# Expert down weights loaded as 16 KB runs, with up and gate products that read every fourth weight column

## The chip, the cores and the metric

One core of a Trainium2 chip runs the whole program; the other cores are idle. The metric is the device time of one execution in microseconds (us), from the first to the last instruction. The core has a matrix engine (TensorE, PE in the profile, with its weight loads as PEld), a vector engine (DVE), a scalar engine (ACT), GpSimd (POOL) and SyncE (SP), which in this kernel issues nearly all transfers from the chip's memory into on-chip memory. A matmul here is called with a stationary operand (loaded into the array first) and a moving operand (streamed past it column by column).

## The reference

Two transformer layers on 256 tokens of width 1024, all in float32. The second one ends in a mixture of 32 experts with two experts for each token. Cut to what matters here:

```python
def expert_block(args):
    xb, e = args                       # tokens of expert e, 1024 wide
    hid = jax.nn.silu(xb @ w1[e]) * (xb @ w3[e])
    return hid @ w2[e]
...
"w1": (32, 1024, 512)   "w3": (32, 1024, 512)   "w2": (32, 512, 1024)     # float32
```

Each matrix of an expert is 2 MB, so the 96 matrices are 192 MB, and every one is read once. The hidden width is 512: hidden unit f is column f of w1 and w3 and row f of w2. The order in which the 512 hidden units are worked through is free as long as the columns of w1 and w3 and the rows of w2 agree on it.

## The kernel before, in words

The dense part of the two layers comes first (to about 690 us). After it the kernel routes the tokens and goes through the 32 experts in 8 quads of 4. For each quad it builds `xg`, the tokens of the four experts (up to 32 slots for each), by products of one-hot matrices with the normed tokens `n3` (line 977). There the stationary operand is `n3[:, tb, c:D:KC]`, which reads every eighth element of a row, 128 of them 32 bytes apart. Then, for each expert, with `places` the three on-chip places of its matrices:

- Lines 997 to 1002: for n = 0 (w1) and n = 1 (w3), 8 blocks c of the input width and 4 groups g of hidden units, a matmul whose stationary operand is 32 columns of `xg` and whose moving operand is a 128x128 piece of the weights. Group g uses its own 32 columns of the array (`tile_position`), and its result goes to its own 32 partitions of `ps`; the four groups run side by side. Each float32 matmul is recorded as two, so a matrix is 64 records of L999.
- ACT takes the silu (L1285), DVE multiplies (L1782), PE turns the result over (L1004), DVE copies it to `hid_T` (L1784).
- Lines 1007 to 1011: the down product with w2, in which block b of four takes the hidden units that group b of the step before has made: 32 records of L1009. ACT and DVE bring the result out (L1288, L1787).

At the end of a quad L1019 weights the results by the gates and puts them back to their tokens, and DVE adds them to `h` (L1793).

The weights come through `expert_load` on SP's queue (line 559), in the order w1, w3, w2 for expert 0, 1, 2 and so on. Expert 2 has places of its own (`third_w`); the others alternate between `even_w` and `odd_w`. SP issues w1 of expert e+2 when the w1 products of expert e are done (`e_w1`), w3 after its w3 products (`e_up`), and w2 after its down products (`e_y`); for expert 3 it waits for expert 0, and for expert 4 for expert 2. From expert 4 on this is the loop `stream`. w1 and w3 put rows 8p to 8p+7 on partition p, 16 KB that lie together in memory. w2 puts rows p, 128+p, 256+p and 384+p on partition p, four runs of 4 KB. An instruction whose weights have not landed waits in order on PE, and all that follows it on PE waits too.

Of the kernel before, what the change touches and what calls it, by code (L numbers as in the profile page):

```python
# [31 lines left out]
P = 128  # L32
# [16 lines left out]
EFF = 512  # L49
SLOTS = 32  # L50
# [206 lines left out]
def layers_kernel(nc, a, table, windows, out):  # L257
# [135 lines left out]
    xg = moe("xg", [P, KC, P])  # L393
# [123 lines left out]
    @block.sync  # L517
    def _(sp):
        def load(u):
            if u >= 3:  # L520
                sp.wait_ge(lo_ready, u - 2)
            kc, cols = units[u]["kc"], units[u]["cols"]
            dst = ring[:, u % 3, 0:kc * cols].rearrange("p (c n) -> p c n", c=kc)
            for c0, c1, src in units[u]["src"]:
                sp.dma_start(dst[:, :, c0:c1], src).then_inc(landed[u % 3], 16)

        for tb in range(TB):
            sp.dma_start(h[:, tb, :], a["x"][0, P * tb:P * tb + P, :]).then_inc(in_x[tb], 16)
        load(0)
        sp.wait_ge(in_rows, 80)  # L530
        load(1)
        sp.dma_start(mem_tok[:, :, :], a["mem"][0].rearrange("(b p) n -> p b n", p=P)).then_inc(in_mem, 16)
        for u in range(2, S2 + 3):
            load(u)

        up_v = a["w_ffn_in"][0].rearrange("(c p) n -> p c n", p=P)
        down_v = a["w_ffn_out"][0].rearrange("(c p) n -> p c n", p=P)
        with sp.Fori(2, NF - 1) as i:
            addresses = [sp.snap(i * UC), sp.snap(i * UC + FF), sp.snap(i * 2 - 2)]
            freed = [sp.snap(i * 3 + (S2 - 3 + j - 2)) for j in range(3)]  # L540
            for j in range(3):
                s = (S2 + j) % 3
                sp.wait_ge(lo_ready, freed[j])
                if j < 2:
                    dst = ring[:, s, :].rearrange("p (c n) -> p c n", c=KC)
                    src = up_v[:, :, bass.ds(addresses[j], UC)]
                else:
                    dst = ring[:, s, :].rearrange("p (c n) -> p c n", c=2)
                    src = down_v[:, bass.ds(addresses[j], 2), :]
                sp.dma_start(dst, src).then_inc(landed[s], 16)  # L550


        w1, w3, w2 = a["w1_2"][0], a["w3_2"][0], a["w2_2"][0]
        sources = (w1.rearrange("e (p c) f -> p e c f", c=KC), w3.rearrange("e (p c) f -> p e c f", c=KC),
                   w2.rearrange("e (c p) n -> p e c n", p=P))

        def expert_load(e, places, which, landing):
            src = sources[which][:, bass.ds(e, 1), :, :].rearrange("p e c n -> p (e c) n")
            sp.dma_start(places[which], src).then_inc(landing, 16)

        for u in range(S2 + 3 * (NF - 2), U):
            if u == second_merge + 2:
                sp.wait_ge(o_done, 20)
                expert_load(0, odd_w, 0, landed_w[1][0])
            elif u in (second_merge + 5, second_merge + 7):
                if u == second_merge + 5:
                    sp.wait_ge(o_done, 28)
                which = (u - second_merge - 3) // 2
                expert_load(0, odd_w, which, landed_w[1][which])
            load(u)  # L570
        sp.wait_ge(merged_ready, 8)
        expert_load(1, even_w, 0, landed_w[0][0])
        sp.wait_ge(lo_ready, U)
        expert_load(1, even_w, 1, landed_w[0][1])
        expert_load(1, even_w, 2, landed_w[0][2])
        sp.wait_ge(unit_done, U)
        for which in range(3):
            expert_load(2, third_w, which, in_third3[which])
        for which in range(3):
            sp.wait_ge((e_w1, e_up, e_y)[which], 1)  # L580
            expert_load(3, odd_w, which, landed_w[1][which])

        def stream(pass_, lo_pair):

            with sp.Fori(lo_pair, EXPERTS // 2) as i:
                for odd in range(2):
                    e = sp.snap(i * 2 + odd)
                    used = sp.snap(i * 2 + (pass_ * EXPERTS + odd - 1))
                    for which in range(3):
                        sp.wait_ge((e_w1, e_up, e_y)[which], used)  # L590
                        expert_load(e, (even_w, odd_w)[odd], which, landed_w[odd][which])

        stream(0, 2)
        sp.wait_ge(passes_ready, 1)
        n_pass = sp.value_load(passes_i[0:1, 0:1], min_val=1, max_val=T // SLOTS)
        with sp.If(n_pass > 1):
            with sp.Fori(1, n_pass) as again:
                stream(again, 0)
            sp.nop()
        for tb in range(TB):  # L600
            sp.wait_ge(fin_ready, tb + 1)
            sp.dma_start(out[0, P * tb:P * tb + P, :], n3[:, tb, :]).then_inc(fin_out, 16)
        sp.wait_ge(fin_out, 32)
# [62 lines left out]
    def _(pe):  # L666
# [190 lines left out]
        for step, *arg in plan:  # L857
# [63 lines left out]
            elif step == "rope":  # L921
# [4 lines left out]
                n = T if r == 0 else 2 * T  # L926
# [40 lines left out]
        def quad_body(q):  # L967

            looped = not isinstance(q, int)
            e0 = pe.snap(q * QUAD) if looped else 0  # L970

            if not looped:
                pe.wait_ge(n3_ready, 2)
            pe.wait_ge(hot_part, q * 2 + 2)
            for c in range(KC):
                for tb in range(TB):
                    last = mm(ps[:, 2 + c // 4, P * (c % 4):P * (c % 4) + P], n3[:, tb, c:D:KC],  # L977
                              one_hot[:, tb, :], start=tb == 0, stop=tb == 1)
            last.then_inc(xg_done, 1)
            pe.wait_ge(hot_ready, q + 1)  # L980
            for tb in range(TB):
                last = nc.tensor.transpose(ps[:, 0, P * tb:P * tb + P], gated_hot[:, tb, :], ident)
            last.then_inc(gt_done, 1)
            pe.wait_ge(xg_part, q + 1)
            pe.wait_ge(xg_ready, q + 1)
            for e in range(QUAD):
                if looped:
                    places, landing = (even_w, odd_w)[e % 2], landed_w[e % 2]
                    arrived = pe.snap(q * 32 + 8 * (e + e % 2))
                else:  # L990
                    places = (odd_w, even_w, third_w, odd_w)[e]
                    landing = (landed_w[1], landed_w[0], in_third3, landed_w[1])[e]
                    arrived = (16, 16, 16, 32)[e]
                done = pe.snap(e0 + e) if looped else e
                for n in range(2):
                    pe.wait_ge(landing[n], arrived)
                    for c in range(KC):
                        for g in range(4):
                            last = mm(ps[SLOTS * g:SLOTS * g + SLOTS, 4 + e % 2, P * n:P * n + P],  # L999
                                      xg[:, c, SLOTS * e:SLOTS * e + SLOTS], places[n][:, c, P * g:P * g + P],  # L1000
                                      start=c == 0, stop=c == KC - 1, tile_position=(0, SLOTS * g))
                    last.then_inc((e_w1, e_up)[n], 1)
                pe.wait_ge(e_hid, done + 1)
                nc.tensor.transpose(ps[:, 6, 0:P], hid[:, :], ident).then_inc(e_T, 1)  # L1004
                pe.wait_ge(landing[2], arrived)
                pe.wait_ge(e_hidT, done + 1)
                for b in range(4):
                    for g in range(4):
                        last = mm(ps[SLOTS * g:SLOTS * g + SLOTS, 7, 0:UC],  # L1009
                                  hid_T[:, SLOTS * b:SLOTS * b + SLOTS], places[2][:, b, UC * g:UC * g + UC],  # L1010
                                  start=b == 0, stop=b == 3, tile_position=(0, SLOTS * g))
                last.then_inc(e_y, 1)

            pe.wait_ge(gt_ready, q + 1)
            pe.wait_ge(e_yA, e0 * 2 + 2 * QUAD)
            pe.wait_ge(e_yD, e0 * 2 + 2 * QUAD)
            for tb in range(TB):
                for half in range(2):
                    last = mm(ps[:, 2 * tb + half, :], gate_T[:, P * tb:P * tb + P],  # L1019
                              y_quad[:, 512 * half:512 * half + 512], start=True, stop=True)  # L1020
                last.then_inc(comb_done, 1)

        quad_body(0)
        pe.wait_ge(passes_ready, 1)
        n_pass = pe.value_load(passes_i[0:1, 0:1], min_val=1, max_val=T // SLOTS)
# [818 lines left out]
```

## Time and profile before

| | |
|---|---|
| median of 3 runs | 1168.72 us (1168.04 to 1173.64) |
| span of the profiled execution | 1168.5 us |
| PE busy | 968.1 us, 83% |
| DVE busy, ACT busy | 525.2 us, 359.5 us |
| moved by DMA | 310.02 MB, 265 GB/s over the span |
| mean granted TensorE clock | 0.933 |

The profiled execution took 1168.5 us from its first to its last instruction, and no other time of it is recorded; that is 0.2 us under the median of the three runs. The busy times are shares of the whole span and say little of one stage: the dense part and the experts have different limits, so the views below are read by stretch. In the rows, "idle before <-" names what ended an engine's idle time before a group of instructions, and the clock is a share of 2.4 GHz.

### The profile page before, as it was taken

Reading aid. Unit: us, or ns where it says so; the run is one execution under the profiler, and the core shown is the slowest. Engines: PE = TensorE matmul, PEld = TensorE weight load, DVE = VectorE, ACT = ScalarE, POOL = GpSimd, SP = SyncE. Lnnn points to the kernel's source line nnn. Section 1 sums busy time; section 2 is a strip of 40 time slices with the busy share of each in tenths; the row PEclk is TensorE's granted clock in tenths of the full one; section 3 lists DMA queues with packets and bytes.
Section 4 is the critical chain, followed back from the end, with each engine's and each line's share of the span. In section 5 each row is a group of like instructions: output and inputs, shape, how many; then the busy total and the mean of one; then the engine's idle time right before and its main releaser. Section 6 shows DMA issues by size and latency. Waiting matters only on the chain.

```text
span 1168.5 us, 23578 instructions
## 1 busy us (share of the span) xinstructions
PE 968.1 (83%) x10387; PEld 854.4 (73%) x10387; DVE 525.2 (45%) x859; ACT 359.5 (31%) x541; POOL 46.3 (4%) x43
## 2 busy tenths in 40 slices
PE   5999999889999997999998877767676767676763
PEld 5999999889999996899987866645454545454542
DVE  4546666756555656778875641212121211111113
ACT  4445546453433335343665421010000000101001
POOL 0100000400000000000210200000000000000000
PEclk8999999989999999999999879999888888988897
DMA  9754423735555553544445886999999999999994
GB/s 331 223 179 145 132 70 97 241 129 190 192 177 196 179 179 118 164 144 155 145 145 185 268 340 260 391 404 421 422 422 424 422 423 422 422 422 422 422 422 167
DMA packets 121376, 310.02 MB, mean 265 GB/s; under 512 B 5636, under 2 KB 92360, under 8 KB 113000
## 3 DMA queue, kind: packets, MB, share of 16 engines
q1 hardware_dynamic: 119568, 304.66, 69.5%
q0 software_dynamic: 1008, 4.20, 1.0%
q8 instruction: 43, 0.70, 0.2%
q10 hardware_dynamic: 744, 0.35, 0.1%
q14 instruction: 13, 0.11, 0.0%
HBM read 308.14 MB, written 1.05 MB: 265 GB/s over the span
## 4 chain that ended last, share of the span: by engine, by line
PE 52%; issue 41%; DVE 3%; ACT 1%; DMA 1%; POOL 1%; ACTq 0%; POOLq 0%; DVEq 0%; SPq 0%
PE ps L671 16%; PE ps L672 15%; PE ps L673 15%; DMA arena<-in_w_proj_b 1%; PE ps L927 1%; DVE w_lo L1322 1%; PE ps L837 1%; PE ps L769 0%; PE ps L825 0%; PE ps L796 0%; DMA rows<-in_g_mix 0%; PE ps L800 0%; PE ps L815 0%; PE ps L804 0%; PE ps L803 0%
## 5 line engine op out<-in xcount | busy, mean ns | idle before, releaser
L671 PE MATMUL ps<-x_hi,w_hi 128*128 128x256 f32 x928 | 268.4, 289 | 0.0
L672 PE MATMUL ps<-x_lo,w_hi 128*128 128x256 f32 x928 | 263.7, 284 | 0.0
L673 PE MATMUL ps<-x_hi,w_lo 128*128 128x256 f32 x928 | 263.6, 284 | 0.0
L1322 DVE TENSOR_TENSOR w_lo<-arena,w_hi 128x2048 fp32r<-128x2048 f32 (+3 forms) x83 | 165.5, 1996 | 60.5 <-ACT w_hi L1064 60.0
L999 PE MATMUL ps<-arena,xg 128*32 128x128 f32 x3968 | 136.1, 298 | 64.3 <-DMA arena<-in_w 56.4
L671 PEld LDWEIGHTS ps<-x_hi,w_hi 128*128 128x128 f32 x928 | 178.1, 192 | 6.5 <-issue 4.9
L999 PEld LDWEIGHTS ps<-arena,xg 128*32 128x32 f32 x3968 | 121.7, 121 | 81.1 <-DMA arena<-in_w 67.9
L672 PEld LDWEIGHTS ps<-x_lo,w_hi 128*128 128x128 f32 x928 | 178.2, 192 | 1.6 <-issue 1.0
L673 PEld LDWEIGHTS ps<-x_hi,w_lo 128*128 128x128 f32 x928 | 178.1, 192 | 0.2
L1064 ACT ACTIVATE w_hi<-arena 128x2048 fp32r<-128x2048 f32 (+3 forms) x83 | 138.4, 1670 | 48.3 <-PE ps L673 26.2
L1782 DVE TENSOR_TENSOR hid<-silu_e,ps 128x128 f32<-128x128 f32 x32 | 9.2, 288 | 189.3 <-ACT silu_e L1285 189.3
L1009 PE MATMUL ps<-arena,hid_T 128*32 128x256 f32 x992 | 70.6, 433 | 26.5 <-DMA arena<-in_w 18.4
L671 PE MATMUL ps<-w_hi,x_hi 128*128 128x256 f32 x256 | 77.1, 301 | 12.2 <-DVE w_lo L1322 11.5
L977 PEld LDWEIGHTS ps<-one_hot,n 128*128 128x128 f32 x256 | 61.8, 337 | 25.1 <-DVE one_hot L1768 23.8
L977 PE MATMUL ps<-one_hot,n 128*128 128x128 f32 x256 | 63.3, 423 | 19.2 <-DVE one_hot L1768 19.2
L672 PE MATMUL ps<-w_lo,x_hi 128*128 128x256 f32 x256 | 75.1, 293 | 0.0
L673 PE MATMUL ps<-w_hi,x_lo 128*128 128x256 f32 x256 | 75.0, 293 | 0.0
L1009 PEld LDWEIGHTS ps<-arena,hid_T 128*32 128x32 f32 x992 | 35.6, 122 | 50.8 <-DMA arena<-in_w 23.1
L1332 DVE TENSOR_TENSOR w_lo<-arena,w_hi 128x2048 fp32r<-128x2048 f32 x24 | 55.0, 2293 | 31.2 <-ACT w_hi L1074 31.2
L1787 DVE COPY y_quad<-ps 32x256 f32<-32x256 f32 x64 | 27.2, 425 | 92.0 <-PE ps L1009 91.0
L1285 ACT ACTIVATE silu_e<-ps 128x128 f32<-128x128 f32 x32 | 8.9, 277 | 179.4 <-PE ps L999 179.4
L1288 ACT ACTIVATE y_quad<-ps 32x256 f32<-32x256 f32 x64 | 23.9, 373 | 124.9 <-PE ps L1009 124.2
(274 smaller groups left out, 1346.7 us busy)
## 6 DMA issues: line engine op xcount, KB each, us to landing
arena<-in_w SPq DMA_DIRECT2D x93, 2048.0 KB, 23.9
arena<-in_w_in SPq DMA_DIRECT2D x43, 1024.0 KB, 5.4
arena<-in_w_ffn_in SPq DMA_DIRECT2D x22, 1024.0 KB, 5.1
arena<-in_w_ffn_out SPq DMA_DIRECT2D x11, 1024.0 KB, 4.9
arena<-in_w_out SPq DMA_DIRECT2D x8, 1024.0 KB, 6.1
third_w<-in_w SPq DMA_DIRECT2D x3, 2048.0 KB, 12.8
arena<-in_w_mem_kv SPq DMA_DIRECT2D x2, 1024.0 KB, 5.8
arena<-in_w_pool_o SPq DMA_DIRECT2D x4, 512.0 KB, 3.3
```

The lines of the kernel that those rows point to most:

```text
L671: mm(dst, l_hi, r_hi, start=start, stop=False)
L672: mm(dst, l_hi, r_lo, start=False, stop=False)
L673: return mm(dst, l_lo, r_hi, start=False, stop=stop)
L837: mm(o[:, 0:T], v[:, 0, :], r[:, 0:T], start=True, stop=False)
L977: last = mm(ps[:, 2 + c // 4, P * (c % 4):P * (c % 4) + P], n3[:, tb, c:D:KC], one_hot[:, tb, :], start=tb == 0, stop=tb == 1)
L999: last = mm(ps[SLOTS * g:SLOTS * g + SLOTS, 4 + e % 2, P * n:P * n + P], xg[:, c, SLOTS * e:SLOTS * e + SLOTS], places[n][:, c, P * g:P * ...
L1009: last = mm(ps[SLOTS * g:SLOTS * g + SLOTS, 7, 0:UC], hid_T[:, SLOTS * b:SLOTS * b + SLOTS], places[2][:, b, UC * g:UC * g + UC], start=b ...
L1064: fn(w_hi[:, u % 3, 0:n], ring[:, u % 3, 0:n], ACT.Copy).then_inc(hi_ready, 1)
L1288: fn(y_quad[SLOTS * e:SLOTS * e + SLOTS, UC * g:UC * g + UC], ps[SLOTS * g:SLOTS * g + SLOTS, 7, 0:UC], ACT.Copy).then_inc(e_yA, 1)
L1322: v.tensor_tensor(w_lo[:, u % 3, 0:n], ring[:, u % 3, 0:n], w_hi[:, u % 3, 0:n].bitcast(F32), ALU.subtract).then_inc(lo_ready, 1)
L1332: v.tensor_tensor(w_lo[:, s, :], ring[:, s, :], w_hi[:, s, :].bitcast(F32), ALU.subtract)\
L1787: v.tensor_copy(y_quad[SLOTS * e:SLOTS * e + SLOTS, UC * g:UC * g + UC], ps[SLOTS * g:SLOTS * g + SLOTS, 7, 0:UC]).then_inc(e_yD, 1)
```

## The change

Two lines. `w2` is loaded with rows 4p to 4p+3 on partition p. Block b of partition p is then row 4p+b, so the hidden units of group g have to be g, g+4, g+8 and so on, and the moving operand of the up and gate products becomes `places[n][:, c, g:EFF:4]`: 128 float32 elements that lie 16 bytes apart.

```diff
         w1, w3, w2 = a["w1_2"][0], a["w3_2"][0], a["w2_2"][0]
         sources = (w1.rearrange("e (p c) f -> p e c f", c=KC), w3.rearrange("e (p c) f -> p e c f", c=KC),
-                   w2.rearrange("e (c p) n -> p e c n", p=P))
+                   w2.rearrange("e (p c) n -> p e c n", c=4))
...
                             last = mm(ps[SLOTS * g:SLOTS * g + SLOTS, 4 + e % 2, P * n:P * n + P],
-                                      xg[:, c, SLOTS * e:SLOTS * e + SLOTS], places[n][:, c, P * g:P * g + P],
+                                      xg[:, c, SLOTS * e:SLOTS * e + SLOTS], places[n][:, c, g:EFF:4],
                                       start=c == 0, stop=c == KC - 1, tile_position=(0, SLOTS * g))
```

No instruction is added, removed or moved on any engine. What changes on SP's queue is the shape of the w2 transfers. This is the piece with expert 1's last two matrices, expert 2's (`third_w_109` to `third_w_111`) and expert 3's; "-" is before, "+" is the change:

```order
-L559 DMA arena<-in_w_2 128x4096 x2
-L559 DMA arena<-in_w_2 128x4x1024
+L559 DMA arena<-in_w_2 128x4096 x3
 L559 DMA third_w_109<-in_w_2 128x4096
 L559 DMA third_w_110<-in_w_2 128x4096
-L559 DMA third_w_111<-in_w_2 128x4x1024
-L559 DMA arena<-in_w_2 128x4096 x2
-L559 DMA arena<-in_w_2 128x4x1024
+L559 DMA third_w_111<-in_w_2 128x4096
+L559 DMA arena<-in_w_2 128x4096 x3
```

Each w2 transfer was 128 partitions of 4 runs of 1024 elements, and becomes 128 runs of 4096 elements, the shape that w1 and w3 have. Its place in the queue is the same.

## Rows read from the trace of the kernel before

**Rows 1.** Busy time by stretch: engines, granted clock, DMA share, GB/s.

```profile
400.00:500.00 100.00, 92.58 (x655) 83.85 (x654) 64.31 (x79) 40.31 (x48) 1.92 (x3) 0.98 0.50 158
900.00:1000.00 100.00, 68.63 (x1114) 52.73 (x1110) 18.11 (x44) 8.62 (x24) 0.00 (x0) 0.88 1.01 422
```

**Rows 2.** DMA packets and SP's queue (q1) from 757 to 1150 us.

```profile
DMA packets 21323, 164.02 MB, mean 417 GB/s; under 512 B 1263, under 2 KB 1263, under 8 KB 14662
q1 hardware_dynamic: 21318, 163.94, 100.4%
```

**Rows 3.** Timeline of PE, 961 to 999 us: start, duration, instructions, idle before.

```profile
961.66 3.53 PE L999 MATMUL ps<-arena,xg 128*32 128x128 f32 x64 [2.97 <-DMA arena<-in_w]
966.57 1.95 PE L999 MATMUL ps<-arena,xg 128*32 128x128 f32 x64 [1.37 <-DMA arena<-in_w]
971.68 3.61 PE L1009 MATMUL ps<-arena,hid_T 128*32 128x256 f32 x32 [2.12 <-DMA arena<-in_w]
...
982.65 7.92 PE L977 MATMUL ps<-one_hot,n 128*128 128x128 f32 x32 [2.60 <-DVE one_hot L1768]
```

**Rows 4.** Timeline of PE, 912 to 940 us.

```profile
912.05 1.93 PE L1009 MATMUL ps<-arena,hid_T 128*32 128x256 f32 x32 [0.47 <-DMA arena<-in_w]
915.07 3.67 PE L1019 MATMUL ps<-y_quad,gate_T 128*128 128x512 f32 x8 [1.09 <-DVE y_quad L1787]
921.34 7.92 PE L977 MATMUL ps<-one_hot,n 128*128 128x128 f32 x32 [2.59 <-DVE one_hot L1768]
930.23 3.70 PE L999 MATMUL ps<-arena,xg 128*32 128x128 f32 x128 [0.76 <-DVE xg L1778]
935.45 1.93 PE L1009 MATMUL ps<-arena,hid_T 128*32 128x256 f32 x32 [0.47 <-DVE hid_T L1784]
937.17 3.71 PE L999 MATMUL ps<-arena,xg 128*32 128x128 f32 x128
```

**Rows 5.** Timeline of PE in the first two quads, 707 to 759 us.

```profile
707.58 3.70 PE L999 MATMUL ps<-arena,xg 128*32 128x128 f32 x128 [0.68 <-ACT xg L1280]
719.40 0.49 PE L999 MATMUL ps<-arena,xg 128*32 128x128 f32 x9 [1.40 <-issue]
727.79 1.50 PE L999 MATMUL ps<-third_w,xg 128*32 128x128 f32 x42 [2.08 <-issue]
734.67 2.38 PE L999 MATMUL ps<-arena,xg 128*32 128x128 f32 x76 [0.44 <-issue]
756.55 3.70 PE L999 MATMUL ps<-arena,xg 128*32 128x128 f32 x128 [0.76 <-DVE xg L1778]
```

**Rows 6.** Busy time by stretch, where SP's queue runs short.

```profile
756.00:758.00 2.00, 1.45 (x53) 1.45 (x57) 0.31 (x1) 0.48 (x2) 0.00 (x0) 1.00 0.80 324
758.00:760.00 2.00, 2.00 (x84) 1.98 (x75) 0.00 (x0) 0.00 (x0) 0.00 (x0) 1.00 0.74 158
760.00:762.00 2.00, 0.81 (x18) 0.34 (x10) 0.58 (x2) 0.28 (x1) 0.00 (x0) 1.00 0.61 221
```

**Rows 7.** The end, 1145 us to the last instruction.

```profile
1145.50 3.35 PE L999 MATMUL ps<-arena,xg 128*32 128x128 f32 x64 [2.96 <-DMA arena<-in_w]
1150.49 1.93 PE L1009 MATMUL ps<-arena,hid_T 128*32 128x256 f32 x32 [0.61 <-DMA arena<-in_w]
```

**Rows 8.** A strided stationary operand (L977), a packed one (L852): ns min/median/max; pace by stretch.

```profile
L977 PEld LDWEIGHTS ps<-one_hot,n x256: 312/337/342, 698.8 to 1109.1; 128*128 128x128 f32 x128
L977 PE MATMUL ps<-one_hot,n x256: 343/404/606, 698.8 to 1109.2; 128*128 128x128 f32 x128
L852 PEld LDWEIGHTS ps<-w_route,n3T x32: 186/193/334, 676.2 to 689.0; 128*128 128x128 f32 x32
L999 PE MATMUL ps<-arena,xg x3968: 270/273/422, 707.6 to 1148.4; 128*32 128x128 f32 x199
698.80:702.00 3.20, 3.20 (x13) 3.20 (x14) 1.03 (x6) 0.00 (x0) 0.00 (x0) 0.50 0.49 198
702.00:706.50 4.50, 4.50 (x20) 4.50 (x20) 0.00 (x0) 0.00 (x0) 0.00 (x0) 0.99 0.00 0
```

## The prediction

> **What bounds the kernel now.** I read the busy times by stretch first. In the dense part, 400 to 500 us, TensorE is busy 92.58 of 100 us and the DMA engines are half idle. In the experts, 900 to 1000 us, it is the reverse: TensorE is busy 68.63 us, and the DMA share is 1.01 at 422 GB/s [rows 1]. The change touches only the experts, so I read on there.
>
> The view of the DMA queues says what the stream is made of. From 757 to 1150 us SP's queue keeps the 16 engines 100.4% busy. 21323 - 14662 = 6661 packets have 8 KB or more: w1 and w3 of 26 experts, 52 transfers of 128 runs of 16 KB, are 6656. 14662 - 1263 = 13399 have 4 KB: w2 of 26 experts in 512 runs is 13312 [rows 2]. So a w2 transfer goes as 512 packets where w1 and w3 go as 128.
>
> The timeline of PE gives the time of each landing, because there PE sits idle until it. w1 lands at 961.66, w3 at 966.57 (4.91 us later), w2 at 971.68 (5.11 us later) [rows 3]. A w2 transfer of the same 2 MB takes 0.20 us more. Four experts take 971.68 - 912.05 = 59.63 us, or 14.91 each, from one fourth w2 to the next [rows 3, 4].
>
> How much room does TensorE have? Where it waits for no landing, a quad costs: 3.02 us from the last down product to L1019, 6.27 to L977, 8.89 to L999, then 6.94 for each of three experts, and 5.22 from the start of the fourth to its down product [rows 4]. The sum is 44.2 us against 59.6 of DMA. The 15.4 us of room is what any extra cost on L999 has to fit into, and a quad has 8 matrices in L999.
>
> Before the stream settles TensorE is the one that others wait for. From 707.58 to 756.55 us none of its idle times in L999 ends with a landing; three end with nothing that the profile shows (1.40 + 2.08 + 0.44 = 3.92 us) [rows 5]. SP may fetch w1 of expert 6 only when L999 has used up w1 of expert 4, about 1.85 us after 756.55. The DMA rate falls to 158 GB/s just then [rows 6]: a deficit against 422 of (98 + 264 + 201)/422 x 2 us = 2.7 us. So the stream's last 26 experts hang on nine matrices of L999: eight of quad 0 and one of quad 1.
>
> **The change, part by part.**
>
> w2 in 16 KB runs. It gets the shape of w1 and w3, so I price it at their interval: -0.20 us each. Of 32 transfers only those behind the restart count, 26: -5.2 us. The bounds are 0 (if the 0.20 comes from something other than the packets) and -6.4 (all 32). The stream has no other gap to close.
>
> The Trainium skill ("DMA: Bandwidth & Descriptors", "Why small descriptors are slow (HBM only)") charges some 3 cycles for each packet beside one for each 32 bytes. As an estimate from that page, four packets of 128 + 3 cycles against one of 512 + 3 is 1.7%, or 0.09 us, where the rows show 0.20; by the page the gain would be 2.3 us. The rows decide.
>
> The strided moving operand. Each of the 64 matrices of L999 is 16 rounds of four concurrent matmul records. Packed, 128 records take 3.70 us, the last about 0.27 of it, so a round takes (3.70 - 0.27)/31 = 0.11 us [rows 4, 8], 0.86 ns a column. No row has a strided moving operand. The nearest is L977, a strided stationary one of the same 128 float32 columns, 32 bytes apart instead of 16. Its weight load lasts 337 ns where the packed one of L852 lasts 193. Its pace, with 0.40 us for the last of 32, is (7.92 - 0.40)/31 = 243 ns [rows 3, 8], more than twice the 110 ns of a packed round. And that pace does not follow the clock: 13 in 3.20 us at 0.50, 20 in 4.50 us at 0.99 [rows 8]. So what limits it is the reading of the operand, not the array. That is why I expect the moving operand to pay too.
>
> Bounds for one round: 110 ns (free), 243 ns (the pace of the row), and 4 x 110 = 440 ns if the four streams compete and a fetch that now serves four neighbouring columns serves one. The nearest row is L977. Its step is twice as wide as ours, so I take from exactly twice the packed round (220 ns) to its own pace (243 ns), and the middle, 231 ns. For a matrix that is 16 x (231 - 110) = +1.94 us; for the ends +1.76 and +2.13.
>
> Does that fit? TensorE's quad becomes 44.2 + 8 x 1.94 = 59.7 us, DMA's 59.63 - 4 x 0.20 = 58.8. It no longer fits: the limit is (58.8 - 44.2)/8 = 1.82 us for a matrix. TensorE becomes the bound, barely, and the DMA saving is lost. Summed along TensorE alone, with d the extra for a matrix:
>
> - start of quad 1: 756.55 + 8d
> - six quads to the start of quad 7: 6 x (44.2 + 8d)
> - to the last down product: 3 x 6.94 + 5.22 + 8d = 26.0 + 8d
> - the end behind it, unchanged: 1168.5 - 1150.49 = 18.0 [rows 7]
>
> The sum is 1065.8 + 64d. With d = 1.94 that is 1190.0; the ends give 1178.4 and 1202.1. Part of the 3.92 us of unexplained gaps in quad 0 may vanish under longer matmuls. I take off half: 1188. The two buffers for each matrix do not run dry before that: at a quad's first w1 TensorE is 3.02 + 6.27 + 8.89 + 3.7 = 21.9 us behind the last w2, while two experts, 29.4 us of transfers, are still queued.
>
> The low end of the cost is set by DMA: 1168.5 + 9 x 1.76 - 5.2 = 1179.1, or 1175 without the gaps. What follows an L999 group (L1285, L1782, L1004) moves with it. At the very end, w3's last products have to be through before w2 lands. Now PE waits 0.61 us for that landing [rows 7]; the sums hold this. No addition, copy or semaphore changes.
>
> **Rivals.**
>
> *The stride is free (0.30).* For it: 0.86 ns a column is two cycles at 2.4 GHz, which may leave room to fetch, and 16 bytes is half of L977's step. Against it: L977 has the same room and still pays. Then only the packets count: 1168.5 - 5.2 = 1163.3. This is the case on the other side, and it decides where the nine early matrices cost less than the packets give: 9d < 5.2, d < 0.58 us, a round under 146 ns. The Trainium skill ("SBUF — State Buffer", "Door 1: The DMA port swizzle") speaks of 16-byte lines and says "how far you can stride for free depends on dtype: 4 fp32". Read literally a step of four is still free and this rival holds. The same note wants two hits on each line, which a step of four does not give; no row here has this step, and L977's agrees only that a wider one costs.
>
> *The streams compete (0.12).* For it: four groups read at once, and L977 reads alone. Against it: nothing in the trace shows such a limit on packed reads. A round of 440 ns gives d = 5.28 and 1065.8 + 64 x 5.28 = 1404 us.
>
> *A mild cost (0.08).* d between 0.2 and 1.4: TensorE's quad stays under DMA's and only quad 0 and the restart pay, 1168.5 + 9d - 5.2, so 1165 to 1176.
>
> *Neither edit shows (0.04).* The packets don't set the 0.20 and the stride is free: 1168.5.
>
> **How the numbers follow.** My forecast, a doubled or slightly more than doubled round, has 0.46, and 1175 to 1212 for its own range (1212 is a round of 254 ns, from adding L977's extra 144 ns). With the free case and the mild one that is 0.84; the range is 1161 to 1212 and leaves out the competing streams. The measurement tells about 0.5%, 5.8 us, from no change. The free case, at -5.4 against the median, lies at that bound: I split it 0.13 faster, 0.17 same. The mild case is 0.06 same, 0.02 slower; the one without effect 0.04 same. The forecast gives 0.45 slower and 0.01 same, the competing streams 0.12 slower. That is 0.13, 0.28 and 0.59. The sums are made against the span of 1168.5 us, 0.2 under the median.
>
> **What the profile of the changed kernel would show.** Packets under 8 KB between 757 and 1150 us gone but for about 1300, and w2 landing 4.9 us after w3 wherever PE waits for both. If the forecast holds, 64 records of L999 take about 3.8 us at the full clock and nearly the same at the lower one; L1004's wait for `hid` is unchanged; quad 1's first L999 starts near 770 us instead of 756.55; waits of L999 for landings nearly vanish after quad 2; the DMA share in the experts falls a little under 1. If 64 records still take 1.95 us, the free case is right. If they take 7 us, the streams compete. The forecast is wrong if a moving operand is fetched further ahead than a stationary one, or if a step of 16 bytes is not yet the step that costs.

## The result and the profile after

The changed kernel is slower: 1187.43 us median (1185.33 to 1190.03) against 1171.18, ratio 1.0146, 95% interval 1.0125 to 1.0167. (1171.18 is the median of four runs of the kernel before: the three of its table and a fourth at 1173.95.) Its profiled execution took 1187.64 us with a span of 1185.8, 17.3 over the span of before. A time of a run lies about 1.8 us above its span here and in every other run that has both on record. So the span of 1168.5 of before belongs to a time near 1170.3, by that difference, and isn't a time to set beside 1168.72.

The timeline of PE over one settled quad, the answer to [rows 3, 4], shows where that comes from:

```profile
827.10 7.56 PE L999 MATMUL ps<-arena,xg 128*32 128x128 f32 x128 [0.76 <-DVE xg L1778]
...
868.73 1.93 PE L1009 MATMUL ps<-arena,hid_T 128*32 128x256 f32 x32 [0.47 <-DVE hid_T L1784]
871.75 3.67 PE L1019 MATMUL ps<-y_quad,gate_T 128*128 128x512 f32 x8 [1.09 <-DVE y_quad L1787]
878.03 7.92 PE L977 MATMUL ps<-one_hot,n 128*128 128x128 f32 x32 [2.60 <-DVE one_hot L1768]
886.91 7.55 PE L999 MATMUL ps<-arena,xg 128*32 128x128 f32 x128 [0.75 <-DVE xg L1778]
895.96 1.93 PE L1009 MATMUL ps<-arena,hid_T 128*32 128x256 f32 x32 [0.47 <-DVE hid_T L1784]
```

The two matrices of an expert take 7.55 us in L999 where they took 3.70. L1019, L977 and L1009 take what they took. And no row names a landing any more: L1009 waits for `hid_T`, L977 for `one_hot`. The view of PE's waits from 757 to 1168 us says the same for all quads:

```profile
PE ps L1004 <- DVE hid L1782: 19.9, 28, 0.7
PE ps L977 <- DVE one_hot L1768: 18.0, 7, 2.6
PE ps L1009 <- DVE hid_T L1784: 13.3, 28, 0.5
PE ps L1019 <- DVE y_quad L1787: 6.5, 6, 1.1
PE ps L999 <- DVE xg L1778: 5.3, 7, 0.8
```

Before, the longest waits of L999 and L1009 were for landings [rows 3]; the same view of the kernel before, from 757 to 1150 us, has 74.2 us of them in all:

```profile
PE ps L999 <- DMA arena<-in_w: 56.4, 27, 3.0
PE ps L1009 <- DMA arena<-in_w: 17.8, 13, 2.2
```

Here there is none. TensorE sets the pace. From 900 to 1000 us it is busy 83.47 us instead of 68.63 [rows 1]; the DMA rate did not fall there, because the two now need nearly the same time for a quad:

```profile
900.00:1000.00 100.00, 83.47 (x1150) 59.11 (x1143) 18.00 (x45) 8.05 (x23) 0.00 (x0) 0.98 1.00 425
```

The DMA view from 757 to 1150 us, the answer to [rows 2], shows the 4 KB packets gone and the queue no longer full (97.9% for 100.4%):

```profile
DMA packets 11103, 161.73 MB, mean 412 GB/s; under 512 B 1232, under 2 KB 1232, under 8 KB 1232
q1 hardware_dynamic: 11097, 161.63, 97.9%
```

The first two quads and the last down product, the answer to [rows 5 to 7]: timeline of PE, and then busy time by stretch.

```profile
707.76 7.52 PE L999 MATMUL ps<-arena,xg 128*32 128x128 f32 x128 [0.68 <-ACT xg L1280]
718.52 7.57 PE L999 MATMUL ps<-arena,xg 128*32 128x128 f32 x128
767.32 7.56 PE L999 MATMUL ps<-arena,xg 128*32 128x128 f32 x128 [0.76 <-DVE xg L1778]
...
1167.80 1.93 PE L1009 MATMUL ps<-arena,hid_T 128*32 128x256 f32 x32 [0.47 <-DVE hid_T L1784]
```

```profile
764.00:766.00 2.00, 2.00 (x10) 2.00 (x10) 0.00 (x0) 0.00 (x0) 0.00 (x0) 1.00 0.33 139
766.00:768.00 2.00, 1.24 (x18) 0.80 (x21) 0.69 (x1) 0.87 (x2) 0.00 (x0) 1.00 0.00 0
768.00:770.00 2.00, 2.00 (x40) 1.44 (x36) 0.00 (x0) 0.00 (x0) 0.00 (x0) 1.00 0.00 0
770.00:772.00 2.00, 2.00 (x43) 1.50 (x36) 0.00 (x0) 0.00 (x0) 0.00 (x0) 1.00 0.00 0
```

Quad 1 starts L999 at 767.32 instead of 756.55, and the DMA engines stand still for over 6 us, until its first matrix is used up and the next w1 can be issued, where before the rate only dipped to 158 GB/s. The idle times of quad 0 that ended with nothing the profile shows are gone.

### The profile page after: what moved, and what is told of

Same layout as the page of the kernel before. It is cut to its first block, busy times and chain, and to the rows that moved or that the text cites. A ratio compares the mean times of both kernels' runs of the same rounds, so it can differ in the third digit from the quotient of the medians.

```text
span 1185.8 us, 23578 instructions
## 1 busy us (share of the span) xinstructions
PE 1057.4 (89%) x10387; PEld 904.9 (76%) x10387; DVE 525.2 (44%) x859; ACT 359.7 (30%) x541; POOL 46.4 (4%) x43
## 4 chain that ended last, share of the span: by engine, by line
PE 52%; issue 42%; DVE 3%; ACT 1%; DMA 1%; POOL 1%; ACTq 0%; POOLq 0%; DVEq 0%; SPq 0%
PE ps L671 16%; PE ps L672 15%; PE ps L673 15%; DMA arena<-in_w_proj_b 1%; PE ps L927 1%; DVE w_lo L1322 1%; PE ps L837 1%; PE ps L769 0%; PE ps L825 0%; PE ps L796 0%; DMA rows<-in_g_mix 0%; PE ps L800 0%; PE ps L815 0%; PE ps L804 0%; PE ps L803 0%
## 5 line engine op out<-in xcount | busy, mean ns | idle before, releaser
L999 PE MATMUL ps<-arena,xg 128*32 128x128 f32 x3968 | 235.4, 409 | 6.0 <-DVE xg L1778 5.3
L999 PEld LDWEIGHTS ps<-arena,xg 128*32 128x32 f32 x3968 | 171.2, 127 | 62.6 <-issue 6.9
L977 PEld LDWEIGHTS ps<-one_hot,n 128*128 128x128 f32 x256 | 61.8, 336 | 25.1 <-DVE one_hot L1768 23.8
L977 PE MATMUL ps<-one_hot,n 128*128 128x128 f32 x256 | 63.3, 425 | 19.2 <-DVE one_hot L1768 19.2
L1009 PE MATMUL ps<-arena,hid_T 128*32 128x256 f32 x992 | 60.0, 381 | 14.7 <-DVE hid_T L1784 14.7
L671 PEld LDWEIGHTS ps<-w_hi,x_hi 128*128 128x128 f32 x256 | 51.7, 202 | 14.5 <-DVE w_lo L1322 12.1
L1074 ACT ACTIVATE w_hi<-arena 128x2048 fp32r<-128x2048 f32 x24 | 45.9, 1912 | 49.9 <-PE ps L673 49.9
L1009 PEld LDWEIGHTS ps<-arena,hid_T 128*32 128x32 f32 x992 | 34.9, 109 | 30.8 <-issue 19.7
```

Source lines behind the costliest of these rows:

```text
L671: mm(dst, l_hi, r_hi, start=start, stop=False)
L1009: last = mm(ps[SLOTS * g:SLOTS * g + SLOTS, 7, 0:UC], hid_T[:, SLOTS * b:SLOTS * b + SLOTS], places[2][:, b, UC * g:UC * g + UC], start=b ...
L1074: fn(w_hi[:, s, :], ring[:, s, :], ACT.Copy).then_inc(hi_ready, 1)
```

## The experiments

The theory after the result is the one of the prediction: a moving operand whose float32 elements lie 16 bytes apart takes twice as long, 231 ns a round for 110. That makes L999 1.93 us dearer for a matrix and puts a quad of TensorE just above one of DMA. The rivals: the transfers do it; the four streams collide; the cost depends on where the products stand.

### Each edit alone

`packets_only` keeps the new transfers and the old products:

```diff
-                   w2.rearrange("e (c p) n -> p e c n", p=P))
+                   w2.rearrange("e (p c) n -> p e c n", c=4))
```

> w2 is loaded in 16 KB runs, the products read packed columns as before (so the hidden units of the down product are taken in the wrong order). Theory: a w2 transfer falls from 5.11 to 4.9 us, TensorE has room, and 26 of them count: 1163.3 us against a span of 1168.5, ratio 0.9955. Rival (the packets do nothing, something else sets the 0.20 us): ratio 1.000, w2 still landing 5.11 us after w3.

Measured: 1165.59 us, ratio 0.9955, interval 0.9937 to 0.9972, over seven runs from 1161.45 (the profiled one) to 1166.70. The timeline of PE:

```profile
960.43 1.96 PE L999 MATMUL ps<-arena,xg 128*32 128x128 f32 x64 [1.35 <-DMA arena<-in_w]
...
965.33 3.36 PE L1009 MATMUL ps<-arena,hid_T 128*32 128x256 f32 x32 [1.90 <-DMA arena<-in_w]
```

w2 lands 965.33 - 960.43 = 4.90 us after w3, where it took 5.11. The transfer half of the change does what the sum said of it.

`stride_only` keeps the old transfers and takes the new products:

```diff
-  ... places[n][:, c, P * g:P * g + P],
+  ... places[n][:, c, g:EFF:4],
```

> The products read every fourth column, w2 is loaded in 4 KB runs as before (hidden units in the wrong order). Theory: TensorE is the bound, so the missing packet saving costs almost nothing: 1186 to 1190 us, ratio 1.015 to 1.018, 64 records of L999 at 3.8 us. Rival (the slowdown comes from the 16 KB transfers, not from the step): L999 back at 1.95 us and the time of before.

Measured: 1188.17 us, ratio 1.0140, interval 1.0116 to 1.0164, and L999 records at a median of 409 ns, as in the change (273 ns before [rows 8]). This is the view by source line of the change:

```profile
L999 PE MATMUL ps<-arena,xg x3968: 387/409/436, 707.8 to 1165.9; 128*32 128x128 f32 x199
```

With or without the saved 0.2 us of each w2 the time is the same: the saving is lost because TensorE, not DMA, ends the quads. The transfers are not the cause.

### Do the streams collide, or does each pay?

`rotated` is the change with each group starting two blocks further on:

```diff
-  xg[:, c, SLOTS * e:SLOTS * e + SLOTS], places[n][:, c, g:EFF:4],
+  xg[:, (c + 2 * g) % KC, SLOTS * e:SLOTS * e + SLOTS], places[n][:, (c + 2 * g) % KC, g:EFF:4],
```

> As the change, but group g starts at block c = 2g and goes round, so that the four concurrent streams read blocks 4 KB apart and never neighbouring columns of the same row. Theory (each stream pays for its own step): as the change, 1187 us, ratio 1.015. Rival (the streams collide because they read the same 16 bytes at nearly the same time): rounds fall back toward 110 ns and the time to about 1163 us, ratio 0.996.

Measured: 1188.30 us, ratio 1.0149, interval 1.0124 to 1.0174. Nothing changes when the streams no longer read neighbouring columns.

`probe_one` adds products of a single stream at the end of each quad, one line for each step (this is step 4; L1019 to L1027 are moving operands with steps 1, 2, 3, 4, 8, L1029 to L1037 stationary ones):

```diff
+            for _ in range(REPS):
+                mm(ps[:, 0, 0:P], gate_T[:, 0:P], y_quad[:, 0:4 * P:4], start=True, stop=True)
```

> The kernel before with probes at the end of each quad, whose results are overwritten: six products of one stream over the whole array for each step of the moving operand (1, 2, 3, 4, 8 elements of float32), and six with a stationary operand of each of these steps and 32 moving columns. Only the pace of the probe records counts, not the time of the kernel. Theory (a read whose step is 16 bytes or more pays, alone or not, on either operand): moving records follow each other at 110 ns for steps 1, 2 and 3 and at 220 to 245 ns for 4 and 8; stationary ones the same. Rival 1 (it takes four concurrent streams): 110 ns for all steps of the moving operand. Rival 2 (the cost grows with the step): 3 dearer than 2, 8 dearer than 4.

The timeline of PE, 12 records a line:

```profile
974.28 1.58 PE L1019 MATMUL ps<-y_quad,gate_T 128*128 128x128 f32 x12 [1.10 <-DVE y_quad L1808]
975.69 1.53 PE L1021 MATMUL ps<-y_quad,gate_T 128*128 128x128 f32 x12
977.06 2.24 PE L1023 MATMUL ps<-y_quad,gate_T 128*128 128x128 f32 x12
979.12 2.93 PE L1025 MATMUL ps<-y_quad,gate_T 128*128 128x128 f32 x12
981.87 2.98 PE L1027 MATMUL ps<-y_quad,gate_T 128*128 128x128 f32 x12
984.67 1.44 PE L1029 MATMUL ps<-gate_T,y_quad 128*128 128x32 f32 x12
985.95 1.92 PE L1031 MATMUL ps<-gate_T,y_quad 128*128 128x32 f32 x12
987.68 2.75 PE L1033 MATMUL ps<-gate_T,y_quad 128*128 128x32 f32 x12
990.24 2.97 PE L1035 MATMUL ps<-gate_T,y_quad 128*128 128x32 f32 x12
993.02 3.04 PE L1037 MATMUL ps<-gate_T,y_quad 128*128 128x32 f32 x12
995.87 4.61 PE L1040 MATMUL ps<-y_quad,gate_T 128*128 128x512 f32 x5
```

From one start to the next, divided by 12, a moving operand of 128 columns costs 118 ns at step 1, 114 at 2, 172 at 3, 229 at 4 and 233 at 8. The stationary one costs 107, 144 (a few long ones: by source line the median weight load is 197 ns there and 192 at step 1), 213, 232 and 238. That is one quad of eight. In another, from 1054.03 us, steps 1 and 2 of the moving operand took 224 and 190 ns at a granted clock of 0.50 and 0.58; the wider steps took the same as here. A single stream pays as much as four, so rival 1 falls. Half of the expectation falls too, and half of rival 2 holds: the cost does not begin at 16 bytes, a step of 12 bytes already pays, but a step of 32 costs hardly more than one of 16 (233 ns for 229).

`probe_four` has the same steps for four concurrent streams:

```diff
+            for r in range(6):
+                for g in range(4):
+                    mm(ps[SLOTS * g:SLOTS * g + SLOTS, 0, 0:P], gate_T[:, SLOTS * g:SLOTS * g + SLOTS],
+                       y_quad[:, g:g + 4 * (P - 1) + 1:4],
+                       start=True, stop=True, tile_position=(0, SLOTS * g))
```

> The kernel before with probes at the end of each quad, whose results are overwritten: six rounds of four concurrent streams, as in L999, for each step of the moving operand (1, 2, 3, 4, 8 elements). Theory (a threshold at 16 bytes, no competition of the streams): rounds of 110 to 117 ns for steps 1, 2 and 3, 231 ns for 4 and for 8. Rival (the streams share something that the step uses up): step 3 already dearer, step 8 dearer than 4.

The view by source line (ns min/median/max, steps 1, 2, 3, 4, 8 in this order; five lines of it, one from each):

```profile
L1019 PE MATMUL ps<-y_quad,gate_T x384: 269/273/297, 740.6 to 1216.9; 128*32 128x128 f32 x192
L1024 PE MATMUL ps<-y_quad,gate_T x384: 274/278/287, 741.9 to 1218.3; 128*32 128x128 f32 x192
L1029 PE MATMUL ps<-y_quad,gate_T x384: 330/343/422, 743.3 to 1220.5; 128*32 128x128 f32 x192
L1034 PE MATMUL ps<-y_quad,gate_T x384: 393/409/434, 745.4 to 1223.3; 128*32 128x128 f32 x192
L1039 PE MATMUL ps<-y_quad,gate_T x384: 411/412/431, 749.2 to 1226.1; 128*32 128x128 f32 x192
```

These are durations of single records, not the time from one round to the next. In quad 0 the first records of steps 1, 2, 3 and 4 start at 740.62, 741.93, 743.33 and 745.39 us, so a round takes 109, 117 and 172 ns at steps 1, 2 and 3, where the single stream took 118, 114 and 172. The durations are 273, 278, 343, 409 and 412 ns: step 3 is halfway and step 8 is no dearer than 4, as with one stream. The 409 ns of step 4 are the 409 of L999 in the change. What was named as a sign of a shared limit, a dearer step 3, turned up, but `probe_one` shows it for one stream, so it is not the sharing.

### Where the strided products stand

`loop_odd`, `loop_strided` and `quad0_strided` apply the change to some experts only. Each loads w2 in the form that its products need:

```diff
-  places[n][:, c, P * g:P * g + P],
+  (places[n][:, c, g:EFF:4] if looped and e % 2 else places[n][:, c, P * g:P * g + P]),    # loop_odd
+  (places[n][:, c, g:EFF:4] if looped == True else places[n][:, c, P * g:P * g + P]),      # loop_strided
+  (places[n][:, c, g:EFF:4] if looped == False else places[n][:, c, P * g:P * g + P]),     # quad0_strided
```

> The change for experts 5, 7, 9 to 31 alone (the odd ones of quads 1 to 7); all others as before. The output is the reference's. Theory: the strided products cost nothing where TensorE has room. A quad has 44.2 + 4 x 1.93 = 51.9 us of TensorE work against 59.6 - 2 x 0.2 = 59.2 us of DMA, so the packets are kept: 13 x 0.20 = 2.6 us, 1165.9, ratio 0.9978. Rival (a strided product costs time wherever it stands): 28 matrices x 1.93 us = 54 us of extra TensorE work would show in part, ratio over 1.005.

Measured: 1166.43 us, ratio 0.9977, interval 0.9965 to 0.9989. Some 54 us of extra TensorE work in 28 matrices cost nothing that shows, and the gain from the transfers is kept. The timeline of PE shows the dear products among the waits (2 x 64 records for an odd expert):

```profile
898.61 3.91 PE L999 MATMUL ps<-arena,xg 128*32 128x128 f32 x64 [2.30 <-DMA arena<-in_w]
903.51 3.85 PE L999 MATMUL ps<-arena,xg 128*32 128x128 f32 x64 [1.00 <-DMA arena<-in_w]
```

> The change for experts 4 to 31 (quads 1 to 7), quad 0 as before. The output is the reference's. Theory: the sum along TensorE with 56 instead of 64 dear matrices, 1065.8 + 56 x 1.93 = 1174 us, ratio 1.0045; quad 1's first L999 starts at 756.5 as before and no L999 waits for a landing after quad 2. Rival (quad 0 costs nothing because nothing is late there): the time of the change, 1186 us.

Measured: 1177.20 us, ratio 1.0072, interval 1.0057 to 1.0088, above the 1.0045 expected. In its profiled execution the way from the first L999 of quad 0 to the last down product takes 1154.49 - 705.54 = 448.95 us:

```profile
705.54 3.70 PE L999 MATMUL ps<-arena,xg 128*32 128x128 f32 x128 [0.68 <-ACT xg L1280]
...
1154.49 1.93 PE L1009 MATMUL ps<-arena,hid_T 128*32 128x256 f32 x32 [0.47 <-DVE hid_T L1784]
```

Before it took 1150.49 - 707.58 = 442.91 [rows 5, 7]. The 6.0 us more are 0.5%, near the sum. The profiled execution is the fastest of the four (1174.32 us); why the others lie up to 5 us higher stays open. The rival, the time of the change, is refuted. No L999 waits for a landing after 757 us, as expected.

> The change for experts 0 to 3 (quad 0) alone, all others as before. The output is the reference's. Theory: quad 1's first L999 starts at 767.3, 10.8 us late, the stream of experts 6 to 31 restarts as much later and nothing gives it back: 1168.5 + 10.8 = 1179.3 us, ratio 1.009. Rival (the later room takes it up, since TensorE waits for landings in each quad from 1 on): 1168.5 us, ratio 1.000.

Measured: 1180.58 us, ratio 1.0103, interval 1.0084 to 1.0122. Its timeline:

```profile
705.81 7.52 PE L999 MATMUL ps<-arena,xg 128*32 128x128 f32 x128 [0.68 <-ACT xg L1280]
...
765.47 3.70 PE L999 MATMUL ps<-arena,xg 128*32 128x128 f32 x128 [0.76 <-DVE xg L1778]
...
1159.17 3.23 PE L1009 MATMUL ps<-arena,hid_T 128*32 128x256 f32 x32 [0.94 <-DMA arena<-in_w]
```

Quad 0 takes 765.47 - 705.81 = 59.66 us for 48.97 before, 10.7 more; over the whole way it is 453.36 - 442.91 = 10.5 more. Nothing is given back, though TensorE waits for landings in every later quad. So eight dear matrices at the front cost 10.5 us and 56 behind them 6.0, together 16.5; the change has 1167.80 - 707.76 = 460.04, 17.1 more. In the change itself quad 0 takes 10.6 more and the 28 experts behind it (1167.80 - 767.32) - (1150.49 - 756.55) = 6.5 more.

### A version that beats both

`step_two` makes the same trade at half the step, with hidden units and rows of w2 that agree:

```diff
-                   w2.rearrange("e (c p) n -> p e c n", p=P))
+                   w2.rearrange("e (h p q) n -> p e h q n", h=2, q=2))
...
-  places[n][:, c, P * g:P * g + P],
+  places[n][:, c, 2 * P * (g // 2) + g % 2:2 * P * (g // 2) + 2 * P:2],
```

> The same trade at half the step: w2 in 8 KB runs (rows 2p, 2p+1 and 256+2p, 257+2p on partition p), products read every second column, 8 bytes apart. Theory, if the cost of a step begins between 8 and 16 bytes: rounds of 110 ns, and 256 packets for 512 save 0.13 us of each w2, so 1168.5 - 26 x 0.13 = 1165, ratio 0.997. Rival (every step pays): rounds of about 230 ns, 1187 us, ratio 1.016. Between them, rounds of 150 to 180 ns would give 1170 to 1176.

Measured: 1167.14 us, ratio 0.9966, interval 0.9952 to 0.9980. The timeline (L1001 is its L999, L1011 its L1009):

```profile
966.04 2.03 PE L1001 MATMUL ps<-arena,xg 128*32 128x128 f32 x64 [1.34 <-DMA arena<-in_w]
...
971.02 3.41 PE L1011 MATMUL ps<-arena,hid_T 128*32 128x256 f32 x32 [1.90 <-DMA arena<-in_w]
...
990.66 3.89 PE L1001 MATMUL ps<-arena,xg 128*32 128x128 f32 x128 [0.76 <-DVE xg L1780]
```

w2 takes 971.02 - 966.04 = 4.98 us, between 5.11 at 4 KB and 4.90 at 16 KB, and a round (3.89 - 0.28)/31 = 116 ns for 110, 0.1 us more for a matrix. By the medians it is ahead of the kernel before and of the change, and of `loop_odd` by less than the two intervals can tell. Its profiled execution is the slowest but one of the twelve, with a span of 1168.9, no shorter than before; there the way from the first up product (709.70 us) to the last down product (1148.14) takes 438.4 us where it took 442.91, but it starts 2.1 us later, and the end takes 20.8 us instead of 18.0.

## Why the prediction was right

The time, 1187.43 us, lies 0.6 from the 1188 forecast, and the likeliest case is the one that happened. That closeness is in part luck: the 1188 is a sum of spans, and a time lies about 1.8 us above its span. Span against span the forecast is 2.2 us too high. Its steps:

- **w2 in 16 KB runs, -5.2 us.** Shown by `packets_only`: 4.90 us for each, and a ratio of 0.9955, which is -5.3 us. The estimate from the Trainium skill ("DMA: Bandwidth & Descriptors", "Why small descriptors are slow (HBM only)") was 2.3 us. The interval of `packets_only`, 3.3 to 7.4 us less, leaves that out, narrowly; the landings say the same, 0.21 us apart against 0.09.
- **A round of 231 ns, +1.94 us a matrix.** Measured (7.56 - 0.41)/31 = 231 ns and (7.56 - 3.70)/2 = 1.93 us. The middle between twice the packed round and L977's pace was a choice; that it hit is partly luck, but the row it leaned on was the right one. The probes show why its wider step did no harm: 16 and 32 bytes cost nearly the same, 229 and 233 ns for a moving operand, 232 and 238 for a stationary one.
- **TensorE becomes the bound, barely.** A quad of 59.7 us was forecast; from 827.10 to 886.91, one quad's first L999 to the next, it is 59.8. `stride_only` shows that the packet saving is lost.
- **Quad 0 and the restart pay, and nothing is given back.** Shown by `quad0_strided`. Here one term was mis-sized: of the 3.92 us of unexplained gaps the forecast took off half. Quad 0 grew by 767.32 - 707.76 - 48.97 = 10.6 us, where 8 x 1.93 = 15.4 were added, so 4.8 vanished, 2.8 more than I took off. That is the term with the wrong size, and it explains the 2.2 us: 2.8 less here, and 0.6 more in the next six quads, which took (1126.25 - 767.32)/6 = 59.82 us each. The gaps cost more than their idle time: the three groups in which they stand (from 714.52, 723.10 and 732.50 us) took 5.37, 6.19 and 4.55 us where a packed one takes 3.70, 5.0 us more in all, and under the longer products nearly all of that vanished. What they wait for is not shown, but the traces hold a hint. They stand at the same places of the program in the kernel before, `packets_only` and `loop_strided`, 128 and 127 matmul records apart (9 + 1 + 32 + 86, then 42 + 1 + 32 + 52), and the DMA queue that the profile calls "instruction" moved five packets of 16 KB from 700 to 745 us, as many as from 757 to 1150. So they may be waits for the program's own code. No run here tests it.
- **The end.** The last down product starts 1185.8 - 1167.8 = 18.0 us before the end, as before.

The rivals: the free stride is refuted by the 409 ns, competing streams by `rotated` and `probe_one`. The rival's line from the Trainium skill ("SBUF — State Buffer", "Door 1: The DMA port swizzle"), that four float32 are a free stride, does not hold for a float32 moving operand: step 4 costs double and step 3 half as much again (229 and 172 ns for 118). The trace agrees with the sentence beside it, that a 16-byte line wants two hits: step 2 has two and costs 114 ns.

Forecast and not borne out: that the DMA share would fall under 1 in the experts. From 900 to 1000 us it is still 1.00 at 425 GB/s, and from 775 to 1150 us 1.00 at 420, where before it was 1.01 at 420. Most of the missing time sits in the pause before 774 us.

## What to carry to other kernels

A layout that makes transfers longer and an operand strided is a trade between two engines. Price both for a whole stage, then look at the room of the engine that gets dearer: 1.93 us for each of 28 matrices was free, for all 64 it cost 17 us. The room has to be counted where it is. Before the transfer stream fills up, the compute chain releases the transfers, and the 10.7 us that quad 0 grew by arrived at the end. Where a permutation can be split, try the smaller step: 8 bytes cost next to nothing here (116 ns a round for 110), and the cost showed from 12 bytes on.

## What the runs showed of the hardware

- The cost of a step fits the number of 16-byte pieces that a moving operand touches. At steps 1, 2, 3, 4 and 8 in float32, 128 columns touch 32, 64, 96, 128 and 128 pieces, and take 118, 114, 172, 229 and 233 ns: from step 3 on, 1.8 ns for a piece; below that the product's own pace of 0.9 ns a column would hide it. That is a fit to five steps of one type, not a mechanism that a run shows. A stationary operand agrees at step 4 and 8, but is dearer at step 3 (213 ns).
- The strided pace hardly follows the granted clock. In `loop_odd` the 64 strided records from 898.61 took 3.91 us with a granted clock of 0.61, those from 903.51 took 3.85 at 1.00:

```profile
898.60:902.50 3.90, 3.90 (x64) 2.58 (x64) 0.00 (x0) 0.00 (x0) 0.00 (x0) 0.61 1.01 429
903.50:907.30 3.80, 3.79 (x64) 2.17 (x64) 0.00 (x0) 0.00 (x0) 0.00 (x0) 1.00 1.00 427
```

Packed ones took 3.53 us at a granted clock of 0.54 and 1.95 at 1.00 [rows 3]. The strided products lost 0.06 us to the lower clock, the packed ones 1.58.
- Four concurrent streams with a step of 16 bytes do not slow each other: a record has a median of 409 ns in L999 and in the single stream of `probe_one`, and 231 ns for a round stand against 229 for a record of the single stream.
